# GpSimd's low parts of a pair's raw blocks without the wait for VectorE's low part of h

## The reference

```python
def swiglu(x, w_gu, w_down):
    gate, up = jnp.split(x @ w_gu, 2, axis=-1)
    return (jax.nn.silu(gate) * up) @ w_down
...
    for l in range(DEPTH):
        n = norm_g[l]
        x = x + 0.5 * rmsnorm(swiglu(rmsnorm(x, n[0]), w1_gu[l], w1_down[l]), n[1])
        m, S_a, S_r = mixer(rmsnorm(x, n[2]), pos, w_in[l], w_a2[l], b_a[l], gn_gla[l], gn_ret[l], w_out[l],
                            s_gla[l], s_ret[l])
        x = x + rmsnorm(m, n[3])
        x = x + 0.5 * rmsnorm(swiglu(rmsnorm(x, n[4]), w2_gu[l], w2_down[l]), n[5])
```

## Time and profile before

| | |
|---|---|
| median of 3 runs | 2168.72 us (2167.69 to 2168.77) |
| the profiled execution | 2166.24 us |
| its span | 2164.4 us |
| TensorE busy | 2114.4 us, 98% |
| VectorE busy | 1316.5 us, 61% |
| ScalarE busy | 970.9 us, 45% |
| GpSimd busy | 866.5 us, 40% |
| mean granted TensorE clock | 0.996 |

### The profile page before, as it was taken

One profiled execution on the slowest core, in us unless ns is written; L12 is line 12 of the kernel. 1 busy time (PEld: TensorE's weight loads), 2 busy tenths in 40 slices (PEclk: granted clock), 3 DMA queues, 4 the chain that ended last, 5 costly groups with the idle time before them and its releaser, 6 DMA issues.

```text
span 2164.4 us, 43008 instructions
## 1 busy us (share of the span) xinstructions
PE 2114.4 (98%) x17095; PEld 2085.2 (96%) x17095; DVE 1316.5 (61%) x1995; ACT 970.9 (45%) x1727; POOL 866.5 (40%) x708
## 2 busy tenths in 40 slices
PE   8999999999999999999999999999999999999998
PEld 8999999999989989999998999999999899899998
DVE  5988700587367898840188885007863788888202
ACT  4455433442354545543354554335424454555333
POOL 3433344443315443344544333453432345333442
PEclk9999999999999999999999999999999999999999
DMA  5234442322234233442423345332222343344422
GB/s 151 81 110 124 148 135 86 92 79 79 63 93 139 74 88 116 124 153 87 117 61 88 109 126 166 114 105 69 79 69 59 96 137 88 89 119 122 154 87 75
DMA packets 389342, 224.54 MB, mean 104 GB/s; under 512 B 9781, under 2 KB 380265, under 8 KB 387881
## 3 DMA queue, kind: packets, MB, share of 16 engines
q1 hardware_dynamic: 372208, 213.19, 33.6%
q10 hardware_dynamic: 16952, 8.81, 1.4%
HBM read 200.41 MB, written 21.56 MB: 103 GB/s over the span
## 4 chain that ended last, share of the span: by engine, by line
PE 89%; DVE 5%; issue 3%; ACT 2%; POOL 1%; DMA 0%; DVEq 0%; SPq 0%; POOLq 0%; ACTq 0%
PE ps L711 54%; PE ps L770 29%; PE ps L945 1%; DVE x L1991 1%; DVE y L1985 1%; POOL w_lo L636 1%; DVE xs_lo L1745 0%; DVE w_lo L1848 0%; PE ps L1107 0%; PE ps L1124 0%; PE ps L1019 0%; DMA x_tok<-in_x_prompt_dram 0%; ACT o_hi L1624 0%; ACT xs_hi L1286 0%; PE ps L1046 0%
## 5 line engine op out<-in xcount | busy, mean ns | idle before, releaser
L636 POOL TENSOR_TENSOR w_lo<-raw,w_hi 128x384 fp32r<-128x384 f32 (+1 forms) x452 | 558.6, 1246 | 683.7 <-ACT w_hi L1313 683.7
L1313 ACT ACTIVATE w_hi<-raw 128x384 fp32r<-128x384 f32 (+1 forms) x452 | 247.7, 559 | 461.9 <-PE ps L711 451.7
L770 PE MATMUL ps<-xb,w_hi 128*128 128x272 f32 x2048 | 388.1, 288 | 2.4 <-DVE w_lo L1848 2.2
L711 PE MATMUL ps<-xs_hi,w_hi 128*128 128x288 f32 (+1 forms) x1568 | 345.0, 292 | 5.0 <-DVE xs_lo L1745 4.2
L711 PE MATMUL ps<-xs_hi,w_lo 128*128 128x288 f32 (+1 forms) x1568 | 340.5, 288 | 0.0
L711 PE MATMUL ps<-xs_lo,w_hi 128*128 128x288 f32 (+1 forms) x1568 | 339.6, 288 | 0.0
L770 PEld LDWEIGHTS ps<-xb,w_hi 128*128 128x128 f32 x2048 | 321.4, 188 | 4.1 <-DVE w_lo L1848 4.1
L770 PE MATMUL ps<-xb,w_lo 128*128 128x272 f32 x1024 | 295.3, 288 | 0.0
L711 PEld LDWEIGHTS ps<-xs_hi,w_hi 128*128 128x128 f32 x1568 | 257.2, 188 | 12.2 <-DVE xs_lo L1745 6.2
L711 PE MATMUL ps<-h_hi,w_lo 128*128 128x256 f32 x1272 | 267.2, 289 | 0.0
L711 PE MATMUL ps<-h_lo,w_hi 128*128 128x256 f32 x1272 | 266.1, 288 | 0.0
(11 more groups left out here) (264 smaller groups left out, 3805.3 us busy)
## 6 DMA issues: line engine op xcount, KB each, us to landing
raw<-in_w_gu_dram SPq DMA_DIRECT2D x176, 512.0 KB, 4.2
raw<-in_w_in_dram SPq DMA_DIRECT2D x56, 512.0 KB, 3.8
raw<-in_w_down_dram SPq DMA_DIRECT2D x64, 384.0 KB, 3.4
raw<-in_w_down_dram SPq DMA_DIRECT2D x64, 320.0 KB, 3.1
h_away<-low_away SPq DMA_DIRECT2D x44, 272.0 KB, 4.5
h_lo<-h_away SPq DMA_DIRECT2D x8, 1088.0 KB, 8.4
raw<-in_w_out_dram SPq DMA_DIRECT2D x16, 512.0 KB, 4.0
ret_state<-in_state_ret_dram SPq DMA_DIRECT2D x8, 512.0 KB, 6.6
```

Of the source, the lines that this page charges most:

```text
L636: pool.tensor_tensor(lo, raw[:, u, k0:k0 + n, :], hi.bitcast(F32), ALU.subtract)\
L711: mm = pe.matmul(bank_part(bank, a), w, v[:, k, TOK[a]], start=(start and n == 0), stop=(stop and n == 2))
L770: mm = pe.matmul(ps[:, j, 0:TH], w[j][:, k, :], xb[:, c_, part, k, :], start=(k == 0 and m == 0), stop=(k == KH - 1 and m == 2))
L1313: act.activation(hi, raw[:, u, k0:k0 + n, :], ACT.Copy).then_inc(hi_split, 1)
```

## The change

In GpSimd's list, the wait before each (n,6) is taken out. (n,6) then waits only for ScalarE's high part. Nothing else is changed.

```diff
                     for n, j in POOL_LOWS:
-                        if j == 6:
-                            wait(pool, h_ready, l, f * KF + TILE0 + n - 1)
                         term_low(l, f, n, j)
```

## The result

The changed kernel takes 2333.2 us (median of 4 runs, 2332.76 to 2335.14) against 2168.24 us before: ratio 1.0763, 95% interval 1.0744 to 1.0781. The profiled execution's span is 2331.6 us, 167.2 more than before. The forecast was 2302 us, range 2235 to 2345: the direction and the place were right, the size 31 us short.

The account below looks back on a forecast made before the run. TensorE was taken to bound the pair phase, VectorE close behind. Window 1's 0.9 plus 32.5 us for windows 2 to 14 made 33.4 per FFN, 133.6 in four: 2168.72 + 133.6 = 2302 us, range 2235 to 2345.

Parts of the forecast that it names:

- TensorE bounds, VectorE follows with 0.8 us of slack: Pair phase: TensorE sets the 10.55 us period; the three-engine loop through VectorE has 0.8 us to spare per pair.
- the middle, 9.75: Loop length without blocks, taken between window 1's 9.62 us and 9.90 us with the settled window's VectorE time.
- Only the four instructions with two SBUF operands suffer: VectorE's product, sum1, sum3 and low contend with GpSimd; instructions with an operand in PSUM lose nothing.
- 1.1 us a block: Each VectorE instruction made to wait for the whole of a GpSimd low part loses 1.1 us.
- Three blocks, because (n+1,0) starts 0.04 us ahead of sum3: Settled windows: sum1, sum3 and low(n-1) each wait for a GpSimd part, 3.3 us in all; chance 0.62.
- two blocks: Rival: sum3 starts ahead of GpSimd's (n+1,0), loop 11.95 us, 76 us in all, 2245 us; chance 0.22.
- The loop 13.05 us, 2.5 over the period: Windows 2 to 14: 9.75 + 3.3 us against the 10.55 us period, costing 32.5 us per FFN.
- Window 1: one block, 0.9 us: Window 1 of each FFN: GpSimd starts first, product loses 0.9 us and TensorE's stall grows by that.
- Earlier loads bring nothing and the new order of SyncE costs nothing: SyncE's loads: an earlier load is worth 0; the later issue moves a microsecond or two, with time to land.
- The clock stays up: The main sum counted no fall of TensorE's granted clock behind the 2.5 us stalls in each window.
- the rival of the clock: The clock falls behind every window's stall, 1.7 us each, 88 us more, 2390 us; chance 0.06.
- VectorE keeps the path: Rival: VectorE's queued instructions follow each other without letting GpSimd in; only window 1's product blocked, 3.6 us, 2172; chance 0.05.

Follow-up runs that it names:

- the steps of the experiments: Kernel before, wait for low(n-1) moved to before (n+1,0): 2182.98 us; to before (n+1,1): 2239.23 us; the changed kernel completes the series.
- the first experiment: Changed kernel with GpSimd's low parts from (1,6) on replaced by a memset of the same tile, after the same wait: 2167.69 us.
- the kernels with two blocks: Kernel before with the wait moved to before (n+1,1), 2239.23 us; changed kernel with an 8-column GpSimd memset delaying (n+1,0)'s low part, 2239.33 us.

## Why the prediction was right where it was, and short by 31 us

- *TensorE bounds, VectorE follows with 0.8 us of slack.* Right; measured 0.9 (10.55 - 9.63, from the steps of the experiments). The loop of window 1, 9.62, was the better value than the middle, 9.75.
- *Only the four instructions with two SBUF operands suffer.* Right: in the changed kernel sum1, sum3 and low take 1.79 to 1.81, and without GpSimd's reads all four are at their old times. Those with an operand in PSUM stay as they were. In the settled windows they no longer lie beside GpSimd; in window 1 sum2 does, from 113.76 beside GpSimd's part of 113.22 to 114.62, and takes 0.69.
- *1.1 us a block.* Right: 10.73, 11.84, 12.94.
- *Three blocks, because (n+1,0) starts 0.04 us ahead of sum3.* Right, by 0.06 us. Luck had a part in it: the margin was 0.04 us, and 0.01 us ahead turned out not to be enough. The chance of 0.22 for two blocks was fair: a memset of 0.1 us makes it two, at 2239 us, where that rival had 2245.
- *The loop 13.05 us, 2.5 over the period.* 12.94 and 2.39: four FFNs of 13 windows make 124 us instead of 130.
- *Window 1: one block, 0.9 us.* Right: product takes 1.57 there (L1875's longest), GpSimd started at 109.78, as worked out, and the stall grew from 3.20 to 4.04 us. The window itself grew by 1.3 us on average, as the clock fell in one FFN more and for longer in another.
- *Earlier loads bring nothing and the new order of SyncE costs nothing.* Right by the first experiment: 2167.69 us.
- *The clock stays up.* Wrong, and this is the missing 31 us. I set the rival of the clock at 0.06 because a stall of 2.5 us "is shorter than that stall" of 3.2. That was an argument from one case in which it fell, with no row of a shorter stall in which it held. The same trace had the clock staying up behind 3.20 us in the first FFN, so the length of a stall alone did not decide it. The stalls turned out at 2.15 us, and the clock fell behind 25 of 52. The rival's price was right per fall (1.5 measured, 1.7 forecast), its count, every window, was not. The missing step of the sum is half of the rival: 25 x 1.5 = 37 us; less the 6 us by which the loop was put too long, 31. That 2333 still lies in the range is owed to the part of a clock loss that the range was drawn to take in, not to the sum.
- *VectorE keeps the path* (2172) is ruled out by the profile after: at product's end GpSimd, waiting, went ahead of the queued sum1, in each of the windows 2 to 14.

## What to carry to other kernels

A wait that looks idle may be keeping two engines apart. Before taking it out, list what the other engine does in the stretch into which the freed work will move, mark the VectorE instructions with two SBUF operands there, and price each meeting in which both are queued at GpSimd's whole instruction less 0.2 us, which is the 1.1 us of this case; then compare the sum with the slack of the loop, not with zero, since the first block may be nearly free and each further one costs in full. And where a change makes TensorE stall in every round (2.15 us of 12.9 here), put falls of the clock into the sum; matmuls of no use that fill the stall took 43 of the 165 us back here.

## What the runs showed of the hardware

- The turns are strict: with both engines queued, the other one goes next at each instruction's end, in each of the windows 2 to 14 of the changed kernel (1.59 us for GpSimd's (n,6), 1.79 to 1.82 for VectorE's three). The Trainium skill (SBUF — State Buffer, Who interferes with whom) has the exclusive lock and that issue order decides; that GpSimd instructions which only write don't contend is there too, and the memset kernel agrees (0.9998 of the time before).
- The order of two starts 0.06 us apart decided over 94 us of the run; 0.01 us ahead by the record was not enough for GpSimd, 0.05 us was.
- The granted clock fell behind a stall of 2.15 us in 25 of 51 windows of 12.94 and 14.45 us, and in windows 2 to 14 of the kernels with two blocks not behind stalls of some 1.06 us (1.43 once). Which stall is followed by a fall is open. Length alone doesn't say: the two shown above are alike, one stall of 2.52 us and one of 3.20 us had none behind them, and the 1.76 us left in window 1 of the kernel with TensorE kept busy had one in three FFNs of four.
